# Delta-rule recurrence: key scaling and scans moved into the levels, logarithm and root ahead of them, TensorE's levels without a loop

## The reference

```python
kk = (k * k_k).reshape(B, S, H, N)
kk = kk / maximum(sqrt(sum(kk * kk, axis=-1)), 1e-12)
k = k * (1 + (a - 1) * k_a)
def step(state, inp):                  # over 1024 tokens
    r_t, w_t, k_t, v_t, kk_t, a_t = inp
    sa = einsum('bhvk,bhk->bhv', state, -kk_t)
    state = state * w_t + sa[..., None] * (kk_t * a_t) + v_t[..., None] * k_t
    return state, einsum('bhvk,bhk->bhv', state, r_t)
mu_y = mean(y); var_y = mean(square(y - mu_y))      # per head
y = (y - mu_y) * rsqrt(var_y + GN_EPS) * gn_g + gn_b
y = (y + sum(r * k * r_k) * v) * g
return y @ w_o
```

## Time and profile before

| | us |
|---|---|
| median of 3 runs | 2908.2 (2899.17 to 2912.09) |
| the profiled execution | 2902.27 |
| its span | 2900.3 |
| TensorE busy | 2758.1 (95%) |
| VectorE busy | 2003.2 (69%) |
| GpSimd busy | 1442.3 (50%) |
| ScalarE busy | 1349.9 (47%) |

### The profile page before, as it was taken

The page is one execution under the profiler, slowest core; times in us unless marked ns, Lnnn a source line. Parts: engine busy times, 40 slices in busy tenths (PEclk is TensorE's granted clock), DMA queues, the critical chain, the costliest instruction groups (busy, mean ns, idle before and its releaser), DMA issues.

```text
span 2900.3 us, 62957 instructions
## 1 busy us (share of the span) xinstructions
PE 2758.1 (95%) x25488; PEld 2193.7 (76%) x25488; DVE 2003.2 (69%) x2870; ACT 1349.9 (47%) x2332; POOL 1442.3 (50%) x961
## 2 busy tenths in 40 slices
PE   8899999999999999999999988888899999999998
PEld 6444566887888888876678877778778788888887
DVE  6687897788787777788034177877647766656667
ACT  5476977144343333436333255455414544334445
POOL 0001000334767667774266555766463577667772
PEclk9899999999999999999999999999999999999999
DMA  9100000722323223231533322222212112111111
GB/s 317 57 1 15 1 2 2 248 79 73 95 73 101 72 87 101 72 102 37 196 131 116 103 68 68 71 68 65 102 45 59 44 44 73 44 43 58 55 47 73
DMA packets 194406, 225.43 MB, mean 78 GB/s; under 512 B 14862, under 2 KB 151649, under 8 KB 194209
## 3 DMA queue, kind: packets, MB, share of 16 engines
q1 hardware_dynamic: 182529, 180.66, 19.9%
q10 hardware_dynamic: 11680, 42.01, 4.0%
HBM read 185.15 MB, written 37.22 MB: 77 GB/s over the span
## 4 chain that ended last, share of the span: by engine, by line
PE 68%; DVE 11%; issue 5%; ACT 4%; POOL 3%; DMA 0%; ACTq 0%; DVEq 0%; SPq 0%; POOLq 0%
PE ps L149 18%; PE ps L150 17%; PE ps L151 17%; DVE uc L1091 2%; PE ps L2305 2%; PE ps L2294 1%; PE ps L2316 1%; PE ps L3880 1%; PE ps L3803 1%; PE ps L3886 1%; PE ps L3892 1%; ACT d_r L2447 1%; DVE rc_kk L3607 1%; PE ps L4027 1%; PE ps L3863 1%
## 5 line engine op out<-in xcount | busy, mean ns | idle before, releaser
L149 PE MATMUL ps<-x_hi,w_hi 128*128 128x512 f32 x1160 | 453.3, 391 | 2.9 <-POOL w_lo L739 2.8
L151 PE MATMUL ps<-x_hi,w_lo 128*128 128x512 f32 x1160 | 451.5, 389 | 0.0
L150 PE MATMUL ps<-x_lo,w_hi 128*128 128x512 f32 x1160 | 451.4, 389 | 0.0
L739 POOL TENSOR_TENSOR w_lo<-w_room,w_hi 128x512 fp32r<-128x512 f32 x188 | 289.8, 1554 | 232.2 <-ACT w_hi L1253 232.2
L739 POOL TENSOR_TENSOR w_lo<-sq_room,w_hi 128x512 fp32r<-128x512 f32 x182 | 285.4, 1579 | 222.2 <-ACT w_hi L1253 222.2
L1091 DVE SCALAR_TENSOR_TENSOR uc<-u,pc,uc 128x1024 f32<-128x1024 f32 x176 | 327.5, 1871 | 25.9 <-ACT uc L1267 15.6
L1079 DVE TENSOR_TENSOR u<-u,ps 128x512 f32<-128x512 f32 x228 | 151.2, 683 | 193.3 <-PE ps L151 168.7
L149 PE MATMUL ps<-g_hi,w_hi 128*128 128x512 f32 x640 | 250.3, 391 | 6.8 <-DVE h L1157 6.8
L149 PEld LDWEIGHTS ps<-x_hi,w_hi 128*128 128x128 f32 x1160 | 217.8, 188 | 50.4 <-POOL w_lo L739 5.8
L151 PEld LDWEIGHTS ps<-x_hi,w_lo 128*128 128x128 f32 x1160 | 217.7, 188 | 45.7
L150 PEld LDWEIGHTS ps<-x_lo,w_hi 128*128 128x128 f32 x1160 | 217.8, 188 | 44.7
(11 more groups left out here) (493 smaller groups left out, 6840.2 us busy)
## 6 DMA issues: line engine op xcount, KB each, us to landing
w_room<-in_f_w_up_dram SPq DMA_DIRECT2D x48, 512.0 KB, 5.0
rwkv_scratch<-rp_stage ACTq DMA_DIRECT2D x48, 512.0 KB, 3.5
sq_room<-in_f_w_up_dram SPq DMA_DIRECT2D x40, 512.0 KB, 4.8
ada_w<-in_ada_w_dram SPq DMA_DIRECT2D x80, 256.0 KB, 2.7
rc_raw<-rwkv_scratch SPq DMA_DIRECT2D x28, 512.0 KB, 3.8
d_ada_w<-in_ada_w_dram SPq DMA_DIRECT2D x24, 512.0 KB, 8.7
d_r<-in_ada_w_dram ACTq DMA_DIRECT2D x24, 512.0 KB, 6.0
sq_room<-in_f_w_down_dram SPq DMA_DIRECT2D x24, 512.0 KB, 4.1
```

Source lines behind the costliest of these rows:

```text
L149: pe.matmul(out, w_hi, x_hi, start=first, stop=False, skip_group_check=skip)
L150: pe.matmul(out, w_hi, x_lo, start=False, stop=False, skip_group_check=skip)
L151: return pe.matmul(out, w_lo, x_hi, start=False, stop=last, skip_group_check=skip)
L739: pool.tensor_tensor(slot_of(k.w_lo, s), src, slot_of(k.w_hi, s).bitcast(F32), ALU.subtract).then_inc(w_lo_done, 1)
```

## The change

TensorE's levels become a Python loop, so all four are in the program one after the other, and `begun` goes. VectorE's half scan of pair `p` + 2 and its `s1` go ahead of max; kk goes to level 1, `s2` to level 2, the second half scan to level 3; VectorE copies `l` at level 4 alone, ScalarE at levels 1 to 3. ScalarE's `ln` and `rs` go ahead of its levels, `log` and `root` to level 2. GpSimd gets two waits: for kk ahead of `squares` and for the second half scan ahead of `gain`; its order stays.

```diff
-    LA_BY_DVE = (2, 4)
+    LA_BY_DVE = (4,)
...
-    def begun(pe):
-        pe.sem_inc(sem["omka"], 1)
-
     def level_pe(pe, p, lv):
         pe.wait_ge(sem["l_sb"][0], lv + 4 * p)
         for i in range(2):
             pe.wait_ge(sem["z_sb"][0], lv * 2 + (10 * p + i - 1))
             pe.wait_ge(sem["l_sb"][1], lv * 2 + (8 * p + i - 1))
-            begun(pe)
             ul_a(pe, i)
         pe.wait_ge(sem["z_sb"][1], lv + 5 * p)
-        begun(pe)
         u_b(pe)
         for i in range(2):
             pe.wait_ge(sem["u_sb"][0], lv * 2 + (10 * p + i - 1))
-            begun(pe)
             z_a_l_b(pe, i)
         pe.wait_ge(sem["u_sb"][1], lv + 5 * p)
         pe.wait_ge(sem["z_sb"][0], lv * 2 + (10 * p + 1))
-        begun(pe)
         z_b(pe)
...
-            with pe.Fori(1, LV[-1]) as lv:
+            for lv in LV[:-1]:
                 level_pe(pe, p, lv)
...
                 pend_act(act, q)
+            if more:
+                for i in range(2):
+                    ln_act(act, q, i)
+                for i in range(2):
+                    rs_act(act, q, i)
             for lv in LV:
...
-                if more and lv in (1, 2):
-                    ln_act(act, q, lv - 1)
-                if more and lv in (3, 4):
-                    rs_act(act, q, lv - 3)
-                if p and lv == 4:
+                if p and lv == 2:
                     log_act(act, p - 1)
                     root_act(act, p - 1)
...
+            if p + 2 < PAIRS:
+                scan_dve(dve, p + 2, 0)
+            if p:
+                for i in range(2):
+                    s1_dve(dve, p - 1, i)
             if more:
                 for i in range(2):
                     max_dve(dve, q, i)
             for lv in LV:
                 for h in range(2):
                     levels_dve(dve, p, lv, h)
-                if p and lv == 1:
+                if more and lv == 1:
                     for i in range(2):
-                        s1_dve(dve, p - 1, i)
+                        kk_dve(dve, q, i)
+                if p and lv == 2:
+                    for i in range(2):
+                        s2_dve(dve, p - 1, i)
+                if p + 2 < PAIRS and lv == 3:
+                    scan_dve(dve, p + 2, 1)
                 if lv in LA_BY_DVE:
                     la_dve(dve, p, lv)
-                if p and lv == 3:
-                    for i in range(2):
-                        s2_dve(dve, p - 1, i)
-            if p + 2 < PAIRS:
-                scan_dve(dve, p + 2, 0)
             if more:
-                for i in range(2):
-                    kk_dve(dve, q, i)
                 bon_dve(dve, q)
-            if p + 2 < PAIRS:
-                scan_dve(dve, p + 2, 1)
             second_dve(dve, p)
...
+            if more:
+                pool.wait_ge(sem["kk"], 2 * q + 2)
             if p:
                 squares(pool, p - 1)
             if more:
                 bonus_key(pool, q)
+            if p + 2 < PAIRS:
+                pool.wait_ge(sem["scan"], 2 * (p + 3))
             if p:
                 gain(pool, p - 1)
```

## The result

The changed kernel takes 2949.7 us (median of 4 runs, 2940.1 to 2951.9), the kernel before 2905.5 on the same chip (2899.2 to 2912.1): ratio 1.014, interval 1.012 to 1.016. It is slower by 1.4%, 10 us above the forecast's 2940 and inside its range.

The account below looks back on a forecast made before the run. TensorE was taken to be held by waits for `rc_bonus` in the tails (19.7 us) and instruction-fetch stops in the levels (8.4 us). Terms +49.4, +15.4 and -31.9 gave +33 us, hence 2940 us; range 2896 to 2968.

Parts of the forecast that it names:

- The levels without a loop: TensorE's eight level stretches: three more levels of fetched instructions a pair outweigh the saved branches and increments, +49.4 us.
- What comes ahead of the levels: VectorE before max: the half scan and the mean's reductions put there make max and the levels start later, +15.4 us.
- The tail: End of each pair: kk and both scans leave it, so the wait for `rc_bonus` and the lower clock go, -31.9 us.
- A: Rival, in levels and tails: instruction fetching keeps up in straight code, -35 us, so 2873 us; chance 0.14.
- B: Rival, in the levels: fetching runs at its best interval, 2.96 us, -10 us in sum, so 2898 us; chance 0.17.
- C: Rival, in the levels: stops leave TensorE idle and its clock falls, +3 us a pair more, 2963 us; chance 0.17.
- D: Rival: GpSimd and VectorE still overlap, so gain could slip into the tail if kk came late; given nothing.

Follow-up runs that it names:

- after_loop: The changed kernel with TensorE's hardware loop over the middle levels and its increments put back, all other edits kept: 2883.9 us, ratio 0.992.
- before_unrolled: The kernel before with only its loop of levels written out, without the increments: 2962.5 us, ratio 1.019.
- after_two: The changed kernel with a loop of two trips, each of two levels written out, increments back: 2910.1 us, ratio 1.000.
- after_loop_quiet: after_loop with GpSimd's k_t of the next pair held back until the half scan ahead of max is done: 2882.2 us, ratio 0.990.
- after_loop_hold: after_loop with GpSimd's k_t of the next pair held until both max of that pair are done: 2880.1 us, ratio 0.990.

## Why the prediction was right, step by step

**The levels without a loop**, forecast +49.4. Right in mechanism, 12 us low. The eight stretches less the wait for max take 235.5 - 16.5 = 219.0 us, 27.4 each where I had 25.8: +61.8.

The 25.8 was 6.1 intervals of 3.83 us, the mean of nine in the trace of before, plus one block at the loop's rate, 2.5. Two sizes in it were off, in opposite ways. Only 31 of the 57 blocks of the stretches lie between two stops, 3.9 a pair and not 6.1; the other 26 took 3.2 us each (219.0 - 135.8 = 83.2). And the 31 average 4.38: the mis-sized term is this interval.

The 17 with the DMA engines quiet at their start average 3.74, so 3.83 was right for them; the 14 at whose start data is being moved average 5.15. An estimate from the two: data beside the fetching cost 14 x 1.4 = 20 us. The prediction left the loads and stores out of the term. In the kernel before, the repeated level of the earlier trace rows ran beside a DMA share of 0.56 and fetched nothing. That data delays the instruction packet is read from the traces and not from a run of its own: in the six versions with the levels written out, 71 intervals have a share of 0.7 or more in their first 1.2 us and 44 of them a packet later than 2.0 us; 131 have a share under 0.3, and 3 of them such a packet. No run moved the loads.

after_loop, before_unrolled and after_two show the cause of the step as a whole, the fetching, by taking it away, adding it alone, and cutting it to a third.

**What comes ahead of the levels**, forecast +15.4. TensorE waited 16.5 us for max, of which seven waits of 0.15 us stood in the kernel before as well. Inside it the scan was too cheap at 2.5 us. VectorE, then GpSimd, in pair 2 of the changed kernel:

```profile
1810.13 3.22 DVE L3583 TENSOR_TENSOR_SCAN rc_cum<-rc_carry,rc_raw 128x512 f32<-128x512 bf16 x1
```

```profile
1809.93 2.34 POOL L3679 TENSOR_TENSOR rc_k_t<-rc_km,rc_odd 128x1024 f32<-128x1024 f32 x1 [3.23 <-PE ps L3846]
```

The scan starts 0.2 us behind k_t, ends 1.08 behind it, and takes 3.22: near what was left of k_t, 2.14, plus most of its 1.21 alone. The prediction cited the Trainium skill, "SBUF — State Buffer", "SBUF: two separate sides", by which whoever starts first holds the port pair for a whole instruction, and worked out 3.2 us by it. The trace agrees, and so do the 1.35 us of the scaling in after_loop_quiet. My own 2.5 was wrong, +4 us in the sum. Pair 0, in the sum with +1.5, waited 0.5 us, and pair 7, in it with +0.5, not at all, which made up for part of it: that the sum of this step came out so near is partly luck.

**The tail**, forecast -31.9, measured -37.7. The steps held: no wait for `rc_bonus`, gain done within the levels, the transposes of `y_n` without a wait (1.09 us at 1845.54). Six of eight tails are at or under 12.2 us where I had 12.8. The half microsecond for a stop was due only in some: straight code at 60 a us does keep pace there.

**The rivals.** A (fetching keeps up) and B (best interval) fell: the shortest level stretch has 26.5 us. With A falls the Trainium skill's advice ("Runtime: NRT & Kernel Launch", "Instruction fetch mechanics") to unroll fully rather than branch: after_loop's 2884 us against 2950 say the opposite for code this dense. C was half true: the clock is 0.83 to 0.95 in seven of eight stretches (the earlier trace rows has 0.92 in pair 4), as C said it would, and TensorE's busy time in them rose from 135.3 to 149.0 us, part of which only took the place of idle time. C's 2963 stood 13 us above the result, the forecast 10 below, so the time does not decide between them. D's worry was for nothing.

**What the sum hid.** Three errors partly cancelled: +12.4 in the levels, +1.1 ahead of them, -5.8 in the tail, so +7.7 in all, on a base that itself scatters by 13 us.

## What to carry to other kernels

- Count the instructions that are not repeated from a loop. Where TensorE's instructions are as short as here (192 matmuls and their weight loads in 3.70 us), a short loop body is worth more than what its branches cost: 6 us of short idles at them were saved, and still 53 to 66 us were lost on balance. Look at what data is moved beside such code as well: an interval whose start met it took 1.4 us more.
- Take a change of several parts apart before it is judged: all of this one but the loop's part made the kernel 0.8% faster, and that part turned it into 1.4% slower. The four versions with the loop of four trips, 2880 to 2884 us, are the best run here and hardly apart.
- A VectorE operation that meets a GpSimd one in SBUF must be looked for again wherever the GpSimd one is moved to: the scan (3.22 us), the small scaling (1.35 instead of 0.18) and kk (3.50 instead of 1.40) paid in turn for the same two GpSimd operations.

## What the runs showed of the hardware

- Between two stops a block of 256 instructions cost 3.4 to 6.6 us. Its packet took about 1.1 us in the instruction queue and TensorE went on 1.2 to 1.5 us after its end; the rest is the time from TensorE's going on to the start of the next packet, 1.1 to 1.7 us with the DMA engines quiet (a share of 0.21 or less) and up to 4.2 where they were moving data (0.78 or more).
- In the changed kernel no packet started within the six waits for max of 0.9 to 3.0 us; the next started 1.1 to 2.5 us after TensorE went on, near the point where it entered its next block of 256, however long the wait had been.
- An operation of 16 elements a partition in SBUF took 1.35 us instead of 0.18 beside a GpSimd operation of 2.35. Two reductions beside that same one (1.25 us together), max beside k_t (0.69) and, in after_loop_hold, two predicated copies out of PSUM beside k_t (1.21 together, as in the changed kernel with GpSimd idle) were not stretched.
- Six increments a level cost 6 us on one kernel without a loop and 23 on another; about half of the latter lies in the tails, at a lower granted clock.
